# A two-layer encoder whose opening is reordered: x and two weight slabs load first, the first projection stands amid the filter steps

## The reference, cut to what matters

```
h = rms_norm(x)
[u_hyena | q | k | v | gates] = h @ W_in              # one projection, ten column chunks
filters: hdn = sin(freq1 * (z @ w_f1 + b_f1)); hdn = sin(freq2 * (hdn @ w_f2 + b_f2))
         kf  = rfft(decay * (hdn @ w_f3))             # depends on weights alone, not on x
y_h = x2 * (h2 (*) (x1 * (h1 (*) v)))                 # u_hyena after a width-3 convolution; (*) by FFT with kf
y_a = differential attention of q, k, v
x = x + (sig(g_h) * (y_h @ P_h) + sig(g_a) * (y_a @ P_a)) @ W_out
x = x + FFN(rms_norm(x))                              # layer 0 dense, layer 1 top-2 of 8 experts
```

## Time and profile before

| | |
|---|---|
| runs | 1517.43, 1518.35, 1520.45 us; median 1518.35 |
| profiled execution, first to last instruction | 1516.0 us |
| mean granted clock of TensorE | 0.983 of full speed |
| matmul on PE, busy | 1438.1 us, 95% |
| DVE, busy | 1186.0 us, 78% |
| ACT, busy | 878.5 us, 58% |
| read from memory | 370.47 MB |

### The profile page before, as it was taken

How to read it: one execution, slowest core, us unless ns; L and a number is a source line. 1 busy time by engine, 2 the same in 40 slices (tenths; PEclk the granted TensorE clock), 3 DMA queues, 4 the chain that set the end, 5 groups by cost and what they waited for, 6 DMA issues and landing times.

```text
span 1516.0 us, 20582 instructions
## 1 busy us (share of the span) xinstructions
PE 1438.1 (95%) x6848; PEld 1171.6 (77%) x6848; DVE 1186.0 (78%) x1249; ACT 878.5 (58%) x944; POOL 40.9 (3%) x53
## 2 busy tenths in 40 slices
PE   5999898999989999888999999999999999999997
PEld 3887677788868877667887887888878878888786
DVE  5978875545458887846988879989889798898896
ACT  4345644434443446434776767767677677676774
POOL 0020001000000110100000000000000000000000
PEclk9999999999999999996999999999999999999999
DMA  8454135765244442332999989989999999999994
GB/s 280 153 189 140 61 108 154 267 194 184 90 166 167 136 155 99 127 117 89 367 314 341 366 292 367 367 291 368 301 355 366 294 368 351 307 365 299 358 368 137
DMA packets 273410, 372.10 MB, mean 245 GB/s; under 512 B 12818, under 2 KB 217166, under 8 KB 272730
## 3 DMA queue, kind: packets, MB, share of 16 engines
q1 hardware_dynamic: 272650, 368.85, 72.8%
q0 software_dynamic: 720, 2.72, 0.6%
HBM read 370.47 MB, written 1.05 MB: 245 GB/s over the span
## 4 chain that ended last, share of the span: by engine, by line
PE 45%; DVE 10%; issue 6%; ACT 3%; DVEq 0%; POOLq 0%; ACTq 0%; POOL 0%
PE bank L1327 14%; PE bank L1329 13%; PE bank L1328 13%; DVE w_lo L893 4%; PE bank L1573 2%; ACT w_hi L617 2%; PE bank L1341 1%; DVE x L1241 1%; DVE ys L882 1%; DVE act_lo L1210 1%; ACT y_hi L811 1%; DVE tmp L882 1%; DVE stat L1106 0%; PE bank L1466 0%; DVE act L1204 0%
## 5 line engine op out<-in xcount | busy, mean ns | idle before, releaser
L893 DVE TENSOR_TENSOR w_lo<-raw,w_hi 128x2048 fp32r<-128x2048 f32 (+2 forms) x382 | 803.2, 2109 | 151.8 <-ACT w_hi L617 145.2
L617 ACT ACTIVATE w_hi<-raw 128x2048 fp32r<-128x2048 f32 (+2 forms) x382 | 674.0, 1768 | 192.8 <-PE bank L1329 192.4
L1327 PE MATMUL bank<-w_hi,hT_hi 128*128 128x512 f32 (+1 forms) x1232 | 491.4, 399 | 13.6 <-DVE w_lo L893 10.1
L1329 PE MATMUL bank<-w_hi,hT_lo 128*128 128x512 f32 (+1 forms) x1232 | 478.3, 388 | 0.0
L1328 PE MATMUL bank<-w_lo,hT_hi 128*128 128x512 f32 (+1 forms) x1232 | 477.6, 388 | 0.0
L1327 PEld LDWEIGHTS bank<-w_hi,hT_hi 128*128 128x128 f32 x1232 | 232.2, 188 | 68.3 <-issue 12.0
L1329 PEld LDWEIGHTS bank<-w_hi,hT_lo 128*128 128x128 f32 x1232 | 232.1, 188 | 46.5
L1328 PEld LDWEIGHTS bank<-w_lo,hT_hi 128*128 128x128 f32 x1232 | 232.6, 189 | 42.6 <-issue 1.0
L1327 PE MATMUL bank<-w_hi,act_hi 128*128 128x512 f32 (+1 forms) x440 | 174.1, 396 | 6.2 <-DVE act_lo L1210 6.2
L1329 PE MATMUL bank<-w_hi,act_lo 128*128 128x512 f32 (+1 forms) x440 | 171.6, 390 | 0.0
L1328 PE MATMUL bank<-w_lo,act_hi 128*128 128x512 f32 (+1 forms) x440 | 171.3, 389 | 0.0
(11 more groups left out here) (210 smaller groups left out, 1057.7 us busy)
## 6 DMA issues: line engine op xcount, KB each, us to landing
raw<-in_w_moe_down SPq DMA_DIRECT2D x160, 512.0 KB, 7.2
raw<-in_w_moe_gate SPq DMA_DIRECT2D x144, 512.0 KB, 6.5
raw<-in_w_moe_up SPq DMA_DIRECT2D x144, 512.0 KB, 7.7
raw<-in_w_in SPq DMA_DIRECT2D x80, 512.0 KB, 4.8
raw<-in_w_dense_down SPq DMA_DIRECT2D x20, 512.0 KB, 4.2
raw<-in_w_dense_gate SPq DMA_DIRECT2D x18, 512.0 KB, 4.1
raw<-in_w_dense_up SPq DMA_DIRECT2D x18, 512.0 KB, 5.0
raw<-in_w_moe_gate SPq DMA_DIRECT2D x34, 256.0 KB, 2.9
```

Source lines behind the costliest of these rows:

```text
L617: nc.scalar.activation(HI[:, split_slot, 0:width], RAW[:, raw_slot, 0:width], ACT.Copy)\
L893: vec.tensor_tensor(LO[:, split_slot, 0:width], RAW[:, raw_slot, 0:width], HI[:, split_slot, 0:width].bitcast(F32), ALU.subtract).then_inc ...
L1327: mm(out_, l_hi, r_hi, start=start, stop=False)
L1329: return mm(out_, l_lo, r_hi, start=False, stop=stop)
```

## The change

x is loaded first, then what `f1` and `f2` need, then `ident`, `par` and the lambdas, then two weight slabs, and only then the other filter parameters, the transform's matrices and the rotary table, ahead of slab 2. `par_loaded` is cut in two semaphores. On ACT the squares of x stand ahead of the two sines, and slab 0 is split right behind them. On DVE the lambdas and the diagonal stand between the two sine arguments. For layer 0 the list begins `ht`, `hf0`, `v`, `ft0` where it began `hf0`, `ht`, `ft0`, `v`; the banks stay. Layer 1 keeps its order.

```diff
+def ordered(layer):
+
+    if layer:
+        return PLAN
+    named = dict(PLAN)
+    return [(step, named[step]) for step in ("ht", "hf0", "v", "ft0")] + PLAN[4:]
...
     def load_parameters(eng, layer):
 
-        for dst, src in ((R["lamv"][:, :, :].rearrange("p a b -> p (a b)"),
-                          lamv_d[layer:layer + 1, :].to_broadcast([P, 4 * DH])),
-                         (R["wf3"][:, :], wf3_d[layer]),
+        for dst, src in ((PAR[:, :], par_d[layer]),
+                         (R["lamv"][:, :, :].rearrange("p a b -> p (a b)"),
+                          lamv_d[layer:layer + 1, :].to_broadcast([P, 4 * DH]))):
+            eng.dma_start(dst, src).then_inc(event("par_loaded", layer), 16)
+
+    def load_filters(eng, layer):
+
+        for dst, src in ((R["wf3"][:, :], wf3_d[layer]),
                          (R["decay"][:, :, :, :].rearrange("p a b c -> p (a b c)"), decay_d),
-                         (R["hyb"][:, :], hyb_d[layer:layer + 1, :]),
-                         (PAR[:, :], par_d[layer])):
-            eng.dma_start(dst, src).then_inc(event("par_loaded", layer), 16)
+                         (R["hyb"][:, :], hyb_d[layer:layer + 1, :])):
+            eng.dma_start(dst, src).then_inc(event("filters_loaded", layer), 16)
...
+        sp.dma_start(X[:, :, :], x_in.rearrange("(p t) d -> p t d", t=TB)).then_inc(sem("x_loaded"), 16)
+        load_hidden(sp, 0)
         sp.dma_start(IDENT[:, :], cst_d[:, 0:P]).then_inc(sem("ident_loaded"), 16)
-        load_hidden(sp, 0)
-        sp.dma_start(X[:, :, :], x_in.rearrange("(p t) d -> p t d", t=TB)).then_inc(sem("x_loaded"), 16)
         load_parameters(sp, 0)
...
             for p, src in enumerate(mixer_slabs(layer)):
+                if layer == 0 and p == 2:
+                    other_loads()
...
             if layer == 0:
-                sine(0, 0)
-                sine(0, 1)
                 act.wait_ge(sem("x_loaded"), 16)
             for i in range(4):
                 if layer:
                     act.wait_ge(event("ffn_added", 0), i + 1)
                 squares(i, "norm_mix")
+            if layer == 0:
+                sine(0, 0)
+                sine(0, 1)
+                split_to(0, stage)
...
             if layer == 0:
-                for j in range(2):
-                    sine_arg(0, f"f{j + 1}", j)
-
-            dve.wait_ge(event("par_loaded", layer), 5 * 16)
+                sine_arg(0, "f1", 0)
+
+            dve.wait_ge(event("par_loaded", layer), 2 * 16)
...
             diagonal("norm_mix", "h_ready")
+            if layer == 0:
+                sine_arg(0, "f2", 1)
+                split_to(0, stage)
...
                 elif step[:2] == "hf":
                     pe.wait_ge(event("sin_done", layer), 2)
-                    pe.wait_ge(event("par_loaded", layer), 5 * 16)
+                    pe.wait_ge(event("filters_loaded", layer), 3 * 16)
                 elif step[:2] == "ft":
                     pe.wait_ge(event("fpm", layer), 2 * int(step[2]) + 2)
+                    if layer == 0:
+                        pe.wait_ge(sem("cst_loaded"), 2 * 16)
```

More of the change, by code:

```diff
@@ L118 @@
 NEXT_HIDDEN = {"mT": ("n1", [4]), "wo1": ("n2", [6])}
+def ordered(layer):
[3 more added lines that the diff above has]
+    return [(step, named[step]) for step in ("ht", "hf0", "v", "ft0")] + PLAN[4:]
 def plan(layer):
     steps = [("f1", [0]), ("f2", [1])] if layer == 0 else []
-    for step in PLAN:
+    for step in ordered(layer):
         if layer + 1 < DEPTH and step[0] in NEXT_HIDDEN:
@@ L460, in put, with other_loads @@
                 sp.dma_start(d, s).then_inc(raw_loaded[slot], 16)
+        sp.dma_start(X[:, :, :], x_in.rearrange("(p t) d -> p t d", t=TB)).then_inc(sem("x_loaded"), 16)
+        load_hidden(sp, 0)
         sp.dma_start(IDENT[:, :], cst_d[:, 0:P]).then_inc(sem("ident_loaded"), 16)
-        load_hidden(sp, 0)
-        sp.dma_start(X[:, :, :], x_in.rearrange("(p t) d -> p t d", t=TB)).then_inc(sem("x_loaded"), 16)
         load_parameters(sp, 0)
-        sp.dma_start(DFT[:, :, :, :, :].rearrange("p a b c d -> p (a b c d)"), dft_d).then_inc(sem("cst_loaded"), 16)
-        sp.dma_start(ROPE[:, :, :, :].rearrange("p a b c -> p (a b c)"), cst_d[:, P:2 * P])\
-            .then_inc(sem("cst_loaded"), 16)
+        def other_loads():
+            load_filters(sp, 0)
+            sp.dma_start(DFT[:, :, :, :, :].rearrange("p a b c d -> p (a b c d)"), dft_d).then_inc(sem("cst_loaded"), 16)
+            sp.dma_start(ROPE[:, :, :, :].rearrange("p a b c -> p (a b c)"), cst_d[:, P:2 * P])\
+                .then_inc(sem("cst_loaded"), 16)
         for layer in range(DEPTH):
@@ L579, in _ @@
                 load_parameters(pool, layer)
+                load_filters(pool, layer)
             rstd(layer, "norm_mix", STAT[:, 0:TB], STAT[:, 4:4 + TB], TB, D)
@@ L659, in _ @@
                 squares(i, "norm_mix")
+            if layer == 0:
+                sine(0, 0)
+                sine(0, 1)
+                split_to(0, stage)
             act.wait_ge(event("lam_sums", layer), 1)
             a.do(nc.scalar.activation(LAM[:, 2:4], LAM[:, 0:2], ACT.Exp), event("lam_exp", layer), 1)
-            for step, _ in PLAN:
+            for step, _ in ordered(layer):
                 if layer + 1 < DEPTH and step in ("wo0", "wo1"):
@@ L1025, in _ @@
                         wait_filled(dve, layer, "ft0", 3)
+                    else:
+                        dve.wait_ge(event("filters_loaded", layer), 3 * 16)
                     for jt in range(2):
@@ L1403, in _ @@
                         pe.wait_ge(event("ffn_added", 0), 4)
-                    if layer == 0:
-                        pe.wait_ge(sem("cst_loaded"), 2 * 16)
                 elif step in ("vT", "x1T", "x2T"):
```

## The result

The changed kernel takes **1529.55 us** (median; 1528.06 to 1530.95), the kernel before in the same group of runs 1519.4 us: ratio 1.0065 [1.0048, 1.0083]. In a second group, with a profile of its own, it was 1531.05 against 1520.07, ratio 1.0074 [1.0061, 1.0087]. It is slower by 10 to 11 us, where +2.8 was forecast with 1524.0 as the upper end.

The account below looks back on a forecast made before the run. TensorE, busy 95% of the span, was taken as the bound. `hf1` starting sooner −2.6, `hf1` at the low clock +3.5, `x1`'s slow start +1.9: +2.8 us, 1521.2 us median; range 1515.6 to 1524.0.

Parts of the forecast that it names:

- The step that failed: TensorE's opening: filter loads, behind x and two slabs, land at 19.0, hidden by `ht`, so they cost `hf0` nothing.
- Rival D: Opening: clock still low when `hf0` starts, or filters come after 19 and it falls; `hf0` takes 7.1; +4.3, 1522.7; chance 0.12.
- the second sine: ScalarE, filter network in the opening: forecast to start at 15.0 and be over at 15.45.
- the first copy of hT: ScalarE, opening: copies of the transposed x start at 18.8, after slab 0's split, table load and exponential.
- the bank as `hf1`'s limit: TensorE ahead of `hf1`: waits for `ft0`'s banks until the butterflies at 43.8, a pause of 5.2 us, at least 3.9.
- `hf1` at the low clock: After the pause `hf1` runs at 1.2 GHz, 7.1 us against 3.6: +3.5 us.
- the rest of the opening handed on to the end: Whole kernel: later stages have no time to make good or lose, so TensorE's shift after the opening reaches the end.
- B: Clock falls in the pause but `hf1` itself raises it: −1.0 us, 1517.3, up to 1519.3; chance 0.16.
- C: Clock stays up through the pause ahead of `hf1`; only the 2.6 us gain is left: 1515.8; chance 0.15.
- E: Plain gain: `hf1` follows `ft0` at 38.6 without waiting for banks, 7.8 us faster, 1510.6; chance 0.02.
- `x1`'s slow start: TensorE after `hf1`: `x1` begins at the low clock and must raise it, losing 1.3 to 2.4, taken as +1.9 us.
- the table load and the exponential: ScalarE, opening: table load of 1.28 and exponential of 0.20, once beside `hf0`, now hold back the transposed x until 18.8.

Follow-up runs that it names:

- The swap on VectorE: Changed kernel with VectorE making `ft0`'s butterflies ahead of `v`'s convolution in the first layer: 1520.4 us, 10.7 us less than the changed kernel in the same group.

## Why the prediction was wrong

**The step that failed** is this one of the part on TensorE: "16.1 − 2.5 + 5.4 = 19.0, so they cost nothing, hidden by `ht`, with nothing to spare". `hf0` started at 22.47. The run with wf alone shows that this wait is the cause of what follows in TensorE: with it mostly gone, `hf0` has its 3.67 and `v` starts at 23.85. The run with both pauses filled shows what made the lateness dear: at the high clock nothing of the 8.2 us is left. The working had two faults. It priced the loads behind the slabs at their time in the kernel before, though the slow stretch of wf, 3 us at 197 GB/s there, is 4 us at 166 and 2 at 285 here: by these windows an estimate of some 3 of the 3.5 us. And it took the landing of three loads as one date, with a margin of nothing, without asking which of them `hf0` reads. Even wf alone let `hf0` start only at 19.49 to 21.15. Why wf takes longer behind the slabs stays open.

**Rival D named the mechanism** ("the filters come after 19 and it falls between"), with 0.12 and a price of +4.3. The price was too small, since it let `hf0` begin at 19: 3.5 us of lateness were missing. With `hf0` at 22.5 and 7.1 long, `v` from 29.6, D's own sum would have been 1.1 earlier − 3.5 = 2.4 later for `hf1`, + 5.4 = +7.8, near the 8.2 of the profile. A margin of zero should have made D at least as likely as the forecast, and the range should have held its late end.

**Right:** x in at 5.8 (5.9), the second sine at 15.5 (15.0), the first copy of hT at 19.16 (18.8), hT_lo over at 23.2; the bank as `hf1`'s limit with a pause of at least 3.9 (4.17); `hf1` at the low clock, +3.5; the rest of the opening handed on to the end. The swap on VectorE shows the pause's cause. Rivals B, C and E fell: every pause of about 4.2 us in the opening had the low clock in it or at most 0.8 us behind it, and `hf1` did not raise it. By the Trainium skill's page "TensorE: Matmul & The Clock Gate" (Part 1, What's actually happening) `hf1` would release the clock itself; it ran low for all of its 7.16 us, and only `x1`'s 128-row products saw it rise, 9.3 us after `hf1` began. The clock's rise during sustained work the trace does show.

**A size off:** `x1`'s slow start cost 1.0 and not 1.9, because the clock came up 2.3 us into it.

**A step that was right by luck:** the table load and the exponential, "now the transposed x waits behind them". ScalarE's copies did, but VectorE's low half of slab 0 held hT_lo as long or longer.

**Median against profile.** The medians are 10.1 and 11.0 us over before, x1 is 8.2 and 8.6 late. One profile is one execution. The changed kernel's second profile, 8.3 late at the end, is of the fastest of its five (1526.21, median 1531.05); the kernel with both pauses filled has a profile as early as before and a median 2.3 us over it, since its profile too is of its fastest execution. The first profile of before is the shorter of that kernel's two, by 1.4 at the end. Beyond the opening's 8.2 to 8.6 some 1 to 2 us in the medians stay open: how often the clock falls in the executions without a profile isn't seen.

## What to carry to other kernels

When loads are moved behind others, take each load's landing by itself, wait at each place only for what is read there, and treat a margin of nothing as a lost bet: here loads that were 3.5 us late, with the pause at the banks that the order itself makes, became 8.2, because TensorE paused and then worked at half pace. When a step is moved ahead of another on one engine, ask what the other engines' order now holds back: freeing `ft0`'s banks ahead of the convolution, four lines, gave back all of the loss in the median, and with the narrower wait the new opening is 0.3% faster than the old one. Two profiles of the same kernel differ here by up to 2.8 us at the same instruction, and the executions of one kernel by 2 to 13.5 us: look up the time of the profiled execution before its shifts are set against a median.

## What the runs showed of the hardware

- `wf`, 64 rows of 8 KB, moves slowly wherever it stands: 197 GB/s in the kernel before, 238 (8 to 11 us) with the filters first, 166 among the slabs, 193 to 213 from GpSimd's queue together with slabs, each time with the DMA engines' busy share near 1. `decay`, 128 rows of the same 8 KB, moves at 397 GB/s right behind it in the kernel before, and the slabs at 380 to 390. So the size of the rows isn't the reason. The number of rows is one difference that is left, and it was not varied.
- The length of the pause alone did not decide whether the clock fell. It fell inside the 64-row products behind pauses of 0.78, 0.98 and 1.65 us (at 51.6, 25.3 and 21.6), and stayed up through them behind 0.51, 0.84, 1.22 and even 2.46. All pauses of 3.3 us or more in the opening, where the clock was up before, had a low clock in them or close behind, and so had pauses of 2.10, 2.25 and 3.01.
- At the low level the 64-row products did not bring the clock back: it stayed at 0.50 for 9.3 us from the restart of TensorE with `hf1`, over 7.16 us of them and 2.2 us of 128-row products. When TensorE restarted with the 128-row products of `v` instead, in the runs with the filters first, the clock was up again 3.1 to 5.5 us later.
